# Mixture-of-experts input rows: quarter rows gathered and transposed in blocks by VectorE, in place of whole rows transposed by TensorE; hidden rows turned between the gate and the up product

## The reference

```python
def hier_moe(x, norm_g, w_rg, w_re, w_gate, w_up, w_down):
    u = rms_norm(x, norm_g)
    # top-1 of 4 groups, top-2 of its 4 experts: weights dense_w over 16 experts
    ...
    h = jax.nn.silu(jnp.einsum('ntd,edf->ntef', u, w_gate)) * jnp.einsum('ntd,edf->ntef', u, w_up)
    h = h * dense_w[..., None].astype(h.dtype)
    return jnp.einsum('ntef,efd->ntd', h, w_down)
```

## Time and profile before

| | |
|---|---|
| time, median of 3 runs | 1412.51 us (1408.84 to 1415.81) |
| the profiled execution, its own time | 1418.34 us |
| its span, first to last instruction | 1416.5 us |
| mean granted TensorE clock | 0.943 of full speed |
| busy share: PE, DVE, ACT, POOL | 93%, 38%, 21%, 12% |
| HBM read, written | 406.31 MB, 29.44 MB |

### The profile page before, as it was taken

How to read it: one execution, slowest core, us unless ns; L and a number is a source line. 1 busy time by engine, 2 the same in 40 slices (tenths; PEclk the granted TensorE clock), 3 DMA queues, 4 the chain that set the end, 5 groups by cost and what they waited for, 6 DMA issues and landing times.

```text
span 1416.5 us, 36477 instructions
## 1 busy us (share of the span) xinstructions
PE 1312.3 (93%) x15444; PEld 1004.0 (71%) x15444; DVE 540.7 (38%) x1274; ACT 297.5 (21%) x715; POOL 168.4 (12%) x202
## 2 busy tenths in 40 slices
PE   6979999999897989999989999999999799999996
PEld 5869999998535767666755655655546799999983
DVE  3740000000375647564756676664025200000005
ACT  2201111111231131313234343434110111111110
POOL 3110000010201111121211111120000100000003
PEclk9979999999997999999989899898998899999998
DMA  8959999998998699999978797974373599999976
GB/s 284 374 194 354 388 390 390 390 389 340 341 357 273 199 330 335 300 358 301 358 245 299 240 335 236 344 250 169 117 282 134 201 380 385 390 389 391 392 305 208
DMA packets 147223, 437.02 MB, mean 309 GB/s; under 512 B 20711, under 2 KB 51304, under 8 KB 138270
## 3 DMA queue, kind: packets, MB, share of 16 engines
q1 hardware_dynamic: 99494, 367.57, 70.1%
q10 hardware_dynamic: 37296, 38.09, 8.4%
q0 software_dynamic: 10320, 29.79, 6.7%
HBM read 406.31 MB, written 29.44 MB: 308 GB/s over the span
## 4 chain that ended last, share of the span: by engine, by line
PE 65%; issue 12%; DVE 9%; DMA 6%; ACT 3%; SPq 3%; ACTq 1%; POOL 1%; DVEq 0%; POOLq 0%
PE PS L1098 12%; PE PS L1102 11%; PE PS L1351 9%; PE PS L1130 6%; PE PS L1135 5%; PE PS L1485 5%; PE PS L1020 3%; PE PS L1391 2%; PE PS L1429 2%; PE PS L1437 2%; PE PS L1449 2%; SPq L680 1%; DMA W<-in_cache_v 1%; DVE KV L2425 1%; DMA KV<-in_cache_k 1%
## 5 line engine op out<-in xcount | busy, mean ns | idle before, releaser
L1102 PE MATMUL PS<-W,KV 128*32 128x128 f32 x3072 | 344.2, 274 | 0.0
L1098 PE MATMUL PS<-W,KV 128*32 128x384 f32 x3072 | 340.9, 490 | 3.2 <-DVE KV L2046 3.2
L1102 PEld LDWEIGHTS PS<-W,KV 128*32 128x32 f32 x3072 | 336.9, 111 | 1.9
L2286 DVE TENSOR_TENSOR KV<-KV,PS 128x384 f32<-128x384 f32 x32 | 17.7, 554 | 481.5 <-PE PS L1116 426.7
L1351 PE MATMUL PS<-W 128*128 128x256 f32 x768 | 178.2, 386 | 1.3 <-ACT KV L1758 1.3
L1351 PEld LDWEIGHTS PS<-W 128*128 128x128 f32 x768 | 144.2, 193 | 30.8 <-issue 8.8
L1130 PE MATMUL PS<-W,KV 128*32 128x384 f32 x1440 | 162.2, 489 | 0.0
L1135 PE MATMUL PS<-W,KV 128*32 128x256 f32 x960 | 162.2, 327 | 0.0
L2425 DVE STREAM_TRANSPOSE KV<-KV 128x1024 f32<-128x1024 f32 x128 | 154.9, 1226 | 7.8 <-DMA KV<-in_cache_k 7.7
L1098 PEld LDWEIGHTS PS<-W,KV 128*32 128x32 f32 x3072 | 150.5, 109 | 4.5 <-DVE KV L2046 4.1
L1135 PEld LDWEIGHTS PS<-W,KV 128*32 128x32 f32 x960 | 95.6, 109 | 14.4
(11 more groups left out here) (306 smaller groups left out, 1512.4 us busy)
## 6 DMA issues: line engine op xcount, KB each, us to landing
W<-in_w_gate SPq DMA_DIRECT2D x32, 2048.0 KB, 14.4
W<-in_w_up SPq DMA_DIRECT2D x32, 2048.0 KB, 15.5
W<-in_w_down SPq DMA_DIRECT2D x32, 2048.0 KB, 14.4
KV<-in_cache_k SPq DMA_DIRECT2D x256, 256.0 KB, 5.4
W<-in_cache_v SPq DMA_DIRECT2D x128, 512.0 KB, 7.7
yd<-KV ACTq DMA_DIRECT2D x30, 288.0 KB, 7.8
W<-in_w_kvf SPq DMA_DIRECT2D x4, 2048.0 KB, 18.2
W<-in_w_kvf ACTq DMA_DIRECT2D x8, 1024.0 KB, 8.6
```

Source lines behind the costliest of these rows:

```text
L1098: pe.matmul(PS[32 * q:32 * q + 32, bank, 0:WIDE], x, w[:, k, 0:WIDE], start=(k == 0), stop=(k == KC - 1), tile_position=(0, 32 * q), skip_ ...
L1102: mm = pe.matmul(PS[CAP:P, bank, P * q:P * q + P], x, w[:, k, WIDE:FF], start=(k == 0 and q == 0), stop=(k == KC - 1), tile_position=(0, C ...
```

## The change

Each row of XS is now stored as four quarters of 256 floats, and within a quarter the elements are permuted (`in_quarters`) so that the 32 elements that belong to one block of 32 partitions lie together. The gather of an expert becomes three indirect DMAs (Q4 = 3), one for each 32 of its 96 rows: each fetches 128 pieces of 1024 bytes, partition 32a + i getting quarter a of row i. The index table therefore has 3 x 16 columns and four times the row number plus a as entries, made by 12 small VectorE operations. VectorE transposes in blocks of 32 x 32 inside SBUF and multiplies by the gain, into two buffers XQ (one is part of V4) in place of the one XT. PE's `x_tr` is gone, and its stream becomes gate(e), h_tr(e - 1), up(e), down(e - 1). The first expert's rows are taken quarter by quarter (`xt_first`). A gather now waits for VectorE's transpose of expert e - 2 (`xg_read`), which runs an expert earlier than `x_tr` did, and `up` waits for `hidden` of the expert before. The path for more than 96 rows to an expert is adapted too; it does not run on these inputs.

```diff
-                pool.wait_ge(sem("routed"), 5 + l * 6)
...
-                        after(pool, sem("xt_tr"), e - 1 + l * NE)
+                        after(pool, sem("xg_read"), e - 1 + l * NE)
                         settled(pool)
-                        pool.indirect_dma_start(out=XG[j][0:CAP, :], out_offset=None, in_=XS,
-                                                in_offset=bass.IndirectOffsetOnAxis(ap=IDX[0:CAP, e:e + 1], axis=0))\
-                            .then_inc(sem(f"xg_in_{j}"), 16)
+                        for q in range(Q4):
+                            if e == 0:
+                                pool.wait_ge(sem("routed"), 5 + q + l * 8)
+                            pool.indirect_dma_start(out=XG[j][:, 2 * P * q:2 * P * q + 2 * P], out_offset=None, in_=XS4,
+                                                    in_offset=bass.IndirectOffsetOnAxis(ap=IDX[:, NE * q + e:NE * q + e + 1], axis=0))\
+                                .then_inc(sem("x0_in" if e + q == 0 else f"xg_in_{j}"), 16)
...
-                            x = XT[:, k, 32 * q:32 * q + 32]
+                            x = XTQ[j][:, q, k, :]
...
+                        after(pe, sem("h_ready"), e + l * NE)
+                        product(3, 3 * j + 1, count, "up", j)
...
                     halves(e, j, 0)
-                    halves(e, j, 1)
                     if not first:
                         h_tr(e - 1)
-                    x_tr(e + 1, 1 - j)
+                    halves(e, j, 1)
                     if not first:
                         down(e - 1, 1 - j)
...
-                x_tr(0, 0)
                 expert(0, 0)
...
+            def in_quarters(t, out):
+
+                r = ROWS[t]
+                return dve.tensor_scalar(out[0:r, :].rearrange("p (a k n) -> p a k n", a=4, k=KC),
+                                         H[0:r, t, :].rearrange("p (a n k) -> p a k n", a=4, k=KC), rs[0:r, t:t + 1], None, ALU.mult)
...
-                dve.tensor_copy(IDX[:, :], PS[:, 7, 2 * P:2 * P + NE]).then_inc(sem("routed"), 1)
+                table = IDX[:, :].rearrange("p (q e) -> p q e", q=Q4)
+                for q in range(Q4):
+                    for a in range(4):
+                        ins = dve.tensor_scalar(table[32 * a:32 * a + 32, q], PS[32 * q:32 * q + 32, 7, 2 * P:2 * P + NE], 4.0, float(a),
+                                                ALU.mult, ALU.add)
+                    ins.then_inc(sem("routed"), 1)
...
-                def xt(e):
-                    dve.wait_ge(sem("xt_tr"), e + 1 + l * NE)
-                    gained(XT, 0, l, CAP).then_inc(sem("xt_ready"), 1)
+                def xt_first():
+
+                    x = XQ[0].rearrange("p (q k n) -> p q k n", q=Q4, k=KC)
+                    g = gains[:, l, :].rearrange("p (k a) -> p k a", a=1).to_broadcast([P, KC, 32])
+                    for q in range(Q4):
+                        own = slice(2 * P * q, 2 * P * q + 2 * P)
+                        if q == 0:
+                            dve.wait_ge(sem("x0_in"), 16 + l * 16)
+                        else:
+                            dve.wait_ge(sem("xg_in_0"), 32 + l * (24 * NE - 16))
+                        then(dve.transpose(XQ[0][:, own], XG[0][:, own]))
+                        ins = dve.tensor_tensor(x[:, q], x[:, q], g, ALU.mult)
+                    ins.then_inc(sem("xt_ready"), 1)
+                    dve.sem_inc(sem("xg_read"), 1)
+
+                def xt(e, j):
+                    dve.wait_ge(sem(f"xg_in_{j}"), 24 * e + 32 - 8 * j + l * (24 * NE - 16 + 16 * j))
+                    after(dve, sem("up_done"), e - 1 + l * NE)
+                    dve.transpose(XQ[j], XG[j][:, 0:Q4 * 2 * P]).then_inc(sem("xg_read"), 1)
+                    dve.wait_ge(sem("xg_read"), e + 1 + l * NE)
+                    x = XQ[j].rearrange("p (q k n) -> p q k n", q=Q4, k=KC)
+                    for q in range(Q4):
+                        g = gains[:, l, :].rearrange("p (k a) -> p k a", a=1).to_broadcast([P, KC, 32])
+                        ins = dve.tensor_tensor(x[:, q], x[:, q], g, ALU.mult)
+                    ins.then_inc(sem("xt_ready"), 1)
...
-                xt(0)
+                xt_first()
+                xt(1, 1)
                 gates(l)
                 hidden(0)
-                xt(1)
+                xt(2, 0)
...
+                with dve.Fori(1, NE - 3, 2) as e:
+                    for j in range(2):
+                        hidden(e + j)
+                        xt(e + j + 2, 1 - j)
```

More of the change, by code:

```diff
@@ L375, in build @@
         XT = V8[:, 4, :].rearrange("p (k n) -> p k n", k=KC)
+        XQ = [a[:, 0:Q4 * 2 * P] for a in (V8[:, 4, :], V4[:, :])]
+        XTQ = [a.rearrange("p (q k n) -> p q k n", q=Q4, k=KC) for a in XQ]
         SG = V8[:, 5, 0:FF]
@@ L1084, in moe, with product @@
             def moe(l):
-                def x_tr(e, j):
-                    k = 8 * e + 16 - 8 * j
-                    pe.wait_ge(sem(f"xg_in_{j}"), k + l * (8 * NE))
-                    after(pe, sem("xt_ready"), e + l * NE)
-                    transposes(XG[j], 0, CAP, KC).then_inc(sem("xt_tr"), 1)
-                def product(bank, slot, count, name):
+                def product(bank, slot, count, name, j):
                     pe.wait_ge(sem(f"w_in_{slot}"), count + l * (8 * NE))
@@ L1145, in halves @@
                         after(pe, sem("silu_done"), e + l * NE)
-                        product(2, 3 * j, count, "gate")
+                        product(2, 3 * j, count, "gate", j)
                     else:
-                        product(3, 3 * j + 1, count, "up")
+                        after(pe, sem("h_ready"), e + l * NE)
+                        product(3, 3 * j + 1, count, "up", j)
                 def expert(e, j):
@@ L1203, in moe @@
                             pe.wait_ge(sem(f"g_xg{l}"), 16 * (n + 1))
-                            transposes(XG[0], 0, P, KC).then_inc(sem(f"g_step{l}"), 1)
+                            for k in range(KC):
+                                for a in range(4):
+                                    at = 2 * P * a + 32 * k
+                                    mm = pe.matmul(PS[32 * a:32 * a + 32, k // 4, (k % 4) * P:(k % 4) * P + P], XG[0][:, at:at + 32], ident,
+                                                   start=True, stop=True, tile_position=(0, 32 * a), skip_group_check=True)
+                            mm.then_inc(sem(f"g_step{l}"), 1)
                             pe.wait_ge(sem(f"g_step{l}"), 9 * n + 2)
@@ L2024, in norm @@
                 norm_scale(phase, t)
+                if phase in ("r0", "r1"):
+                    return in_quarters(t, out)
                 if gain is None:
@@ L2055, in last_row_scaled @@
                 t = NT - 1
-                r = ROWS[t]
-                dve.tensor_scalar(UR[t % 2][0:r, :], H[0:r, t, :], rs[0:r, t:t + 1], None, ALU.mult).then_inc(sem("un_ready"), 1)
+                in_quarters(t, UR[t % 2]).then_inc(sem("un_ready"), 1)
             def router_gains(l, t):
@@ L2294, in moe @@
                 dve.tensor_copy(ONTO[4], PS[0:CAP, 4, FC * CAP:FC * CAP + 64]).then_inc(sem("onto_step"), 1)
-                with dve.Fori(1, NE - 1) as e:
-                    hidden(e)
-                    xt(e + 1)
+                with dve.Fori(1, NE - 3, 2) as e:
+                    for j in range(2):
+                        hidden(e + j)
+                        xt(e + j + 2, 1 - j)
+                hidden(NE - 3)
+                xt(NE - 1, 1)
+                hidden(NE - 2)
                 dve.wait_ge(sem("np_ready"), 1 + l * 1)
```

28 lines of the change are left out of this document (15 added, 13 removed).

## The result

The changed kernel takes 1417.0 us (median of 11 runs, 1413.7 to 1421.2), the kernel before 1412.5 in its 11 beside it: a ratio of 1.0041, 95% interval 1.0021 to 1.0061. That is 0.4% slower, within the 0.5% that counts as the same, where 11 us less were forecast. The profiled execution took 1415.6, its span is 1413.8.

The account below looks back on a forecast made before the run. DMA taken as the experts' bound once TensorE speeds up; down(14) done 4.8 us earlier in layer 0 and 6.4 in layer 1, 11.2 off 1412.51: 1401.3 us. Own range 1394 to 1409; 8 in 10, 1385 to 1422.

Parts of the forecast that it names:

- The gathers in the steady state: Three gather issues per expert on GpSimd, mostly idle; cost only on the DMA, +0.25 us a gather, +3.0 for 12.
- What the pieces cost the DMA: Each expert's gather in 1 KB pieces, taken as packed: two more completions, +0.25 us each, +3.0 for 12; bounds -0.1 and 4.0.
- The DMA as second bound: Expert loads: landings show 18.0 us per expert against TensorE's 17.62, so a faster TensorE uses up the slack and waits.
- The first rival: Experts: TensorE stays the bound, DMA follows a 16.56 us period at 428 GB/s; 27.2 us gained, 1385; chance 0.10.
- x_tr gone: TensorE's eight transposes per expert removed: 1.06 us each expert, 14.8 us over 14; period 17.62 to 16.56.
- The turn at nothing: h_tr(e - 1) moved between gate and up: up(e), 5.3 us, covers ACT's copy, so costed at nothing; uncovered, about 0.5 us.
- The start, +1.7: Start of a layer, index copy to first product: +0.5 index operations, +2.6 later third quarter, -0.5 landing, -0.9 transposes.
- The scaled rows: Strided `in_quarters` reads of H on the chain: +0.25 us each, +1.25 in layer 0 (five), +0.5 in layer 1 (two).
- the upper bound: Scaled rows: at most 0.65 us more each; 2.0 us more in layer 0 and 0.8 in layer 1 than summed.
- The second: Rival: small unpacked pieces cost the DMA time, 1.5 us a gather, 15 us more a layer; 1431; chance 0.20.
- It doesn't do what it says: Rival: a wait takes x_tr's place on TensorE, gate(e) for VectorE or up(e) for `hidden`; under 5%, counted with the last.

Follow-up runs that it names:

- the version of 5: Changed kernel with each third gather in the loop awaiting a gate product, 44 filler transposes before each layer's first expert, VectorE's copies before expert three's transpose: 1375.5 us, 0.977.

## Why the prediction was wrong, point by point

- **The gathers in the steady state: the step that failed.** "Three issues of 1.25 us in place of one on GpSimd, which is idle for most of an expert" was costed on the DMA alone and at nothing for TensorE. Three indirect gathers with 0.30 us between them hold TensorE up 1.1 us per expert in the loop and 4.9 us in the first product. With a pause between them and nothing else the kernel takes 1380.8, 33 us faster than before. The missing term is about 36 us (1417.0 less 1380.8), and it is partly hidden by another error: the DMA as the bound made the forecast 16 us too slow (1401 against the 1385 of TensorE alone). The result inside the wide range, 1385 to 1422, is these two errors of opposite sign and no merit of the mechanism.
- **What the pieces cost the DMA**: +0.25 us each, +3.0 a layer. Packing was right (144 packets). The price had no such effect on the time: from 131 to 300 us the changed kernel moves 401 GB/s where the kernel before moves 388, both at a share of 1.00 to 1.02.
- **The DMA as second bound: fell.** 18.0 us per expert was read off growing landings and taken for a limit. With the pause the DMA carries a period of 16.5 us:

```profile
131.00:300.00 169.00, 169.00 (x2848) 151.44 (x2842) 27.15 (x54) 17.94 (x30) 35.61 (x51) 1.00 1.02 419
```

  TensorE never waits for weights; in the version of 5 the loads from 290 to 330 us take 15.3 to 15.5 us to land (medians), not over 25. The first rival, TensorE stays the bound (1385), is what the mended kernels do. The ceiling of 435 GB/s that the Trainium skill gives (page "DMA: Bandwidth & Descriptors", section "Where 436 GB/s comes from"), weighed there, is in line with 419; its 358 is not.
- **x_tr gone: right**, 1.06 us of period, 17.6 to 16.5, as soon as nothing takes its place. **The turn at nothing: right**, and without it 25 us go.
- **The start, +1.7: too high.** 8.08 us from the first index operation to the first product against 7.91, since a gather of 128 pieces of 1 KB lands in 2.8 us (84.67 less 80.49 was 4.2). But the first product's own length was not in the sum at all, +4.9.
- **The scaled rows, +0.25 each: too low.** The strided form takes 1177 ns, against 754, +0.42 and two thirds of the way to the upper bound. Five of them are +2.1, and the rows below bear it out: from the first one (33.08 before, 32.33 now) to the index operation (79.42 before, 80.67 now) it is 48.3 us against 46.3, +2.0 where +1.25 was summed. That the index operation came exactly 1.25 later is luck: this execution was 0.75 us ahead when the rows began. The upper bound went with the rule on lines of 16 bytes in the Trainium skill, page "SBUF — State Buffer", section "Door 1: The DMA port swizzle"; the trace agrees with its direction.

```profile
L2027 DVE TENSOR_SCALAR V<-H,rs 128x1024 f32<-128x1024 f32 x2 | 2.4, 1177 | 0.1
...
32.33 1.16 DVE L2027 TENSOR_SCALAR KQ<-H,rs 128x1024 f32<-128x1024 f32 x1
...
80.67 2.20 DVE L2208 TENSOR_SCALAR IDX<-PS 32x16 int32<-32x16 f32 x12 [2.10 <-PE PS L1086]
```

- **The rivals.** The second had the sign and the place, the gathers, with another mechanism: they cost TensorE and not the DMA, and 1417 is 14 us under its 1431. "It doesn't do what it says", x_tr's time taken by a wait on TensorE, came closest and was counted under 5%, because only waits on semaphores were thought of. A slip beside it: 0.8 of the forecast and the first rival, 0.65 together, is 0.52 for "faster", not 0.55.

## What to carry to other kernels

When a transfer from GpSimd is split, count its instructions and their spacing, not only bytes and packets, and look at TensorE's timeline for idle time put down to "issue" some 3 us behind the first of them. Three indirect gathers hurt here when they took 3.5 us from the first one's start to the last one's end; two did not, and neither did three in 4.1: move another small operation of GpSimd between them. A busy DMA whose landings grow slowly is no proof of its limit; and where an engine's cover is removed at a stage's start, ask what clock the next product gets.

## What the runs showed of the hardware

Not expected: beside a crowd of indirect transfers TensorE's matmuls come in bursts 0.75 us apart, of about two in the first product and, counting those just behind, of four or five in the run with the gathers under up (203.64, 204.41, 205.12). Without the crowd some 14 start in that time (6 per 0.32 us). In that run it lasts from 3 us after the first gather's start to 0.9 us after the last one's end (203.6 to 205.24 for gathers from 200.85 to 204.33). In the changed kernel TensorE's signals come up to 2 us late as well. What GpSimd and TensorE share here, the supply of instructions, the signals or something below both, is open: no run takes them apart. That a stock of instructions in hand covers the first part is only argued, from the threshold between two and three. One plain transfer among the three did no harm; three plain ones as close weren't tried.
